# Last feed-forward part: seven 2x2 block products in place of eight for 19 of 22 tile pairs, and inner activations in four parts

## The chip, the cores and the metric

The kernel runs on one core of one Trainium2 chip. The metric is the device time of one execution in microseconds (us), the median of the runs shown. The core has TensorE (matrix products, weights loaded beside them), VectorE (DVE), ScalarE (ACT), GpSimd (POOL) and a queue for transfers (SyncE, SP). They run at the same time and each takes its own instructions in order; they wait for each other through semaphores.

## What is computed

The kernel computes two models one after the other on 528 token columns (16 meta tokens and 512 others), later 512 with 256 context tokens: one hybrid layer (feed-forward, retention and attention, feed-forward), then two layers "latent" (0 and 1) with attention and a feed-forward part. The change touches the last feed-forward part, that of latent layer 1, and what feeds it. Cut to this, the reference is

```
def swiglu(x, w_in, w_out):
    a, b = jnp.split(x @ w_in, 2, axis=-1)
    return (jax.nn.silu(a) * b) @ w_out
# h: 512 tokens x 1024; x = modulated layer norm of h; w_in: 1024 x 5632; w_out: 2816 x 1024
# h = layer norm of (h + gate * swiglu(x, w_in, w_out))
```

All products are of float32 values split into a high and a low part: high x high + high x low + low x high, three matmuls for each block of 128 x 128 weights.

## The kernel before, in words

**Layout.** Everything is held transposed, features on the 128 partitions and tokens along the row. Model width 1024 is 8 blocks (k = 0 to 7), the inner width 2816 is 22 tiles (j = 0 to 21). A "pair" j is the tile of a ("fa", then silu) and that of b ("fb", then the gating a*b). The 512 tokens are two halves ("chunks" in the code) of 256 columns, c = 0 and 1. One tile for one half is 8 blocks x 3 matmuls of 256 columns = 24 matmuls (`tile_item`, line 1210, and `mm3`, line 1136, whose three matmuls are lines 1137 to 1139).

**A weight's way.** `SyncE.weight` (3433) loads a tile of 128 x 1024 numbers (512 KB) into one of NW = 4 raw buffers `Wf`; it waits until the buffer's earlier content has been split. `ScalarE.split` (1761, the copy is line 1770) writes the rounded high part into one of six slots (three "base", three "top"), `VectorE.split` (2397, line 2403) subtracts it from the raw weight and writes the low part. Then TensorE may use it. How far ahead ScalarE and VectorE split is `Engine.ahead` (1055): tiles up to `used + look`, only into slots whose earlier tile is finished. Since each engine's instructions are in order, a split stands in its queue at the place where `ahead` gave it out.

**A pair's way.** TensorE makes fa and fb; ScalarE takes silu of fa from PSUM (1971); VectorE multiplies by fb from PSUM (`gated`, 2647, line 2652); ScalarE writes the high part of the result to `H3h` (`hidden_high`, 1980, line 1987); GpSimd subtracts and writes the low part to `H3l` (`PoolE.step`, 3190, line 3197).

**Parts.** The inner activations are kept for 8, 7 and 7 pairs at a time (`CH`, line 20). After each part the 8 output tiles m ("fo") are made, nj blocks each, and VectorE adds them to the residual `H` (`residual`, 2655, line 2664). The part's buffers are used again by the next one. In the first two parts a tile serves both halves in turn; after the third part half 0 gets its 8 output tiles first, then half 1, each with its weights loaded and split anew (`Ffn.ends`, 516).

**Order.** `latent_sequence` (823) makes the list of steps, and `woven` (706) puts the steps of the norms (`chain`, 668) between them by planned times (0.345 us per block). A `Group` (684) gives out the tiles of both halves, the one furthest behind first, with one at most 5 tiles ahead: so half 0 goes ahead while the norm of half 1 is still made. In this layer `look` is 3 throughout. `FILL` (629) puts filler matmuls (line 1125) into known waits of TensorE. The norm in front (b1 and c1) ends with ScalarE's scaled activations `XC` (1948) and high part `X2h` (1951), and low parts `X2l` by VectorE (2628, blocks 0 to 3) and GpSimd (3240, blocks 4 to 7). The norm behind (d1) runs for half 0 during the output tiles of half 1: sums by TensorE (1341, 1363), ScalarE's and VectorE's part, then ScalarE's writes to `H` (1964) and the stores.

PSUM has 8 banks, taken in turn (`take`, 1095); a bank is free once the operation that read it is done.

## Time and profile before

| | |
|---|---|
| median of 3 runs | 3349.62 us (3346.73 to 3352.74) |
| span of the profiled execution, first to last instruction | 3342.8 us |
| difference of the two, what lies around the span | 6.8 us |
| TensorE busy in the profile | 3245.9 us |
| last feed-forward part, first matmul to last | 2936.1 to 3324.3 us |

The profile is of one execution; its times are from the span's start. A group line gives an operation's output and inputs, its shape, how often it occurs, its busy time in total and the mean of one, then the idle time of its engine before it and what ended that. A matmul is recorded with its whole passage (0.28 us); as the next one enters before it is out, they follow each other more closely than that. A few matmul records are missing from the trace. The granted clock is 1.00 at 2.4 GHz and 0.50 at 1.2 GHz.

### The profile page before, as it was taken

To read this page: it belongs to the slowest core of one execution; us is meant where nothing else is said; L and a number is where in the kernel's file an instruction comes from. 1 tells how busy PE (TensorE), PEld (TensorE's weight loads), DVE (VectorE), ACT (ScalarE), POOL (GpSimd) and SP (SyncE) were. 2 spreads that over 40 slices of the span, in tenths; PEclk is the share of its full clock that TensorE was granted. 3 is DMA by queue.
4 is the path that set the end of the run, shared out by engine and by line. 5 is a ranking of instruction groups with operands and counts; after the bars stand their busy time and mean duration, and the time that the engine had idled before them with its cause. 6 is when DMAs were issued, how large, how long until landed. Compare 5 with 4: busy or idle time off the path is not lost. (4 is left out here: it accounts for less than half of the span.)

```text
span 3342.8 us, 59968 instructions
## 1 busy us (share of the span) xinstructions
PE 3245.9 (97%) x24670; PEld 3027.7 (91%) x24686; DVE 1693.8 (51%) x2839; ACT 1329.2 (40%) x2350; POOL 474.2 (14%) x471
## 2 busy tenths in 40 slices
PE   8999999999999999999999999999999999999998
PEld 7999988887778999999789889999998889889997
DVE  4666643546634456665545773222227646743334
ACT  4222222346633432225348663112125547552224
POOL 1010010036400010011013201001010114110100
PEclk9999999999999999999999999999999999999999
DMA  4444422122122344453201421111223212422222
GB/s 162 161 171 171 144 83 70 59 77 60 55 82 95 101 141 169 171 176 110 66 20 42 133 91 64 58 63 58 64 65 125 92 50 54 148 71 95 89 92 92
DMA packets 94973, 325.23 MB, mean 97 GB/s; under 512 B 10800, under 2 KB 15152, under 8 KB 94576
## 3 DMA queue, kind: packets, MB, share of 16 engines
q1 hardware_dynamic: 90992, 307.19, 28.0%
q0 software_dynamic: 3280, 13.68, 1.2%
q8 instruction: 199, 3.26, 0.4%
q14 instruction: 70, 0.57, 0.1%
q10 hardware_dynamic: 432, 0.52, 0.0%
HBM read 309.96 MB, written 2.10 MB: 93 GB/s over the span
## 5 line engine op out<-in xcount | busy, mean ns | idle before, releaser
L2403 DVE TENSOR_TENSOR r_Wbasel<-r_Wf,r_Wbaseh 128x1024 fp32r<-128x1024 f32 (+1 forms) x298 | 380.0, 1277 | 536.3 <-ACT r_Wbaseh L1770 535.9
L1770 ACT ACTIVATE r_Wbaseh<-r_Wf 128x1024 fp32r<-128x1024 f32 (+1 forms) x298 | 307.9, 1037 | 438.8 <-PE PS L1139 340.1
L1137 PE MATMUL PS<-r_X1h,r_Wbaseh 128*128 128x264 f32 (+2 forms) x1216 | 391.0, 322 | 13.0 <-DVE r_X1l L2644 3.7
L1137 PE MATMUL PS<-r_X2h,r_Wbaseh 128*128 128x256 f32 (+1 forms) x1224 | 373.4, 305 | 4.9 <-POOL r_X2l L3240 2.5
L1138 PE MATMUL PS<-r_X1l,r_Wbaseh 128*128 128x264 f32 (+2 forms) x1216 | 377.0, 310 | 0.0
L1139 PE MATMUL PS<-r_X1h,r_Wbasel 128*128 128x264 f32 (+2 forms) x1216 | 376.7, 310 | 0.0
L1139 PE MATMUL PS<-r_X2h,r_Wbasel 128*128 128x256 f32 (+1 forms) x1224 | 366.8, 300 | 0.0
L1138 PE MATMUL PS<-r_X2l,r_Wbaseh 128*128 128x256 f32 (+1 forms) x1224 | 364.1, 297 | 0.0
L2403 DVE TENSOR_TENSOR r_Wtopl<-r_Wf,r_Wtoph 128x1024 fp32r<-128x1024 f32 (+1 forms) x165 | 200.1, 1214 | 274.1 <-ACT r_Wtoph L1770 274.0
L1137 PEld LDWEIGHTS PS<-r_X1h,r_Wbaseh 128*128 128x128 f32 x1216 | 228.9, 188 | 35.7 <-issue 8.1
L1137 PE MATMUL PS<-r_X2h,r_Wtoph 128*128 128x256 f32 x872 | 248.6, 285 | 1.7 <-POOL r_X2l L3240 1.2
L1138 PE MATMUL PS<-r_X2l,r_Wtoph 128*128 128x256 f32 x872 | 248.0, 284 | 0.0
L1139 PE MATMUL PS<-r_X2h,r_Wtopl 128*128 128x256 f32 x872 | 247.9, 284 | 0.0
L1137 PEld LDWEIGHTS PS<-r_X2h,r_Wbaseh 128*128 128x128 f32 x1224 | 230.4, 188 | 18.3 <-POOL r_X2l L3240 3.3
L1138 PEld LDWEIGHTS PS<-r_X1l,r_Wbaseh 128*128 128x128 f32 x1216 | 229.4, 189 | 13.9 <-issue 2.4
L1138 PEld LDWEIGHTS PS<-r_X2l,r_Wbaseh 128*128 128x128 f32 x1224 | 232.3, 190 | 10.4 <-issue 2.6
L1139 PEld LDWEIGHTS PS<-r_X1h,r_Wbasel 128*128 128x128 f32 x1216 | 229.5, 189 | 12.5
L1139 PEld LDWEIGHTS PS<-r_X2h,r_Wbasel 128*128 128x128 f32 x1224 | 229.6, 188 | 7.8
L1770 ACT ACTIVATE r_Wtoph<-r_Wf 128x1024 fp32r<-128x1024 f32 (+1 forms) x165 | 168.4, 1025 | 164.7 <-PE PS L1139 84.0
L1977 ACT ACTIVATE r_TM<-PS 128x256 f32<-128x256 f32 (+1 forms) x198 | 75.8, 384 | 339.4 <-PE PS L1139 334.7
L1137 PE MATMUL PS<-r_X1h,r_Wtoph 128*128 128x264 f32 (+1 forms) x672 | 190.7, 284 | 4.9 <-DVE r_Wtopl L2403 4.9
L2652 DVE TENSOR_TENSOR r_TM<-r_TM,PS 128x256 f32<-128x256 f32 (+1 forms) x198 | 83.3, 420 | 213.6 <-PE PS L1139 202.4
(428 smaller groups left out, 9058.3 us busy)
## 6 DMA issues: line engine op xcount, KB each, us to landing
r_Wf<-in_wmod SPq DMA_DIRECT2D x96, 512.0 KB, 3.6
r_Wf<-in_f_in SPq DMA_DIRECT2D x88, 512.0 KB, 4.4
r_Wf<-in_g_in SPq DMA_DIRECT2D x88, 512.0 KB, 3.5
r_Wf<-in_g_out SPq DMA_DIRECT2D x56, 448.0 KB, 3.3
r_Wf<-in_w_o SPq DMA_DIRECT2D x40, 512.0 KB, 4.4
r_Wf<-in_f_out SPq DMA_DIRECT2D x32, 448.0 KB, 4.2
r_Wf<-in_f_out SPq DMA_DIRECT2D x16, 512.0 KB, 4.4
r_Wf<-in_w_v SPq DMA_DIRECT2D x16, 512.0 KB, 3.5
```

What stands on the lines that cost most here:

```text
L1137: self.e.matmul(o, wh, xh, start=first, stop=False)
L1138: self.e.matmul(o, wh, xl, start=False, stop=False)
L1139: return self.e.matmul(o, wl, xh, start=False, stop=last)
L1770: e.activation(p.w(i, cols)[0], p.Wf[:, i % NW, 0:cols], ACT.Copy).then_inc(*p.hi.did(i))
L1977: e.activation(f.tm(c), p.psb(p.bank(("fa", f.tag, j, c)), f.chunks[c][1]), ACT.Silu).then_inc(*p.act.did(("silu", f.tag, j, c)))
L2403: e.tensor_tensor(l, p.Wf[:, i % NW, 0:cols], h.bitcast(F32), ALU.subtract).then_inc(*p.lo.did(i))
L2652: e.tensor_tensor(x, x, p.psb(p.bank(("fb", f.tag, j, c)), f.chunks[c][1]), ALU.mult).then_inc(*p.dve.did(("gated", f.tag, j, c)))
```

## The change

**Products.** For pairs 3 to 21 of this part the weights of a pair are taken as a 2x2 block matrix: A11 and A12 are the halves of the tile of a (k 0 to 3 and 4 to 7), A21 and A22 those of b. In the code the second load is called B where it is summed (B[:, 0:512] is A21, B[:, 512:1024] is A22). The activations are a 2x2 block matrix as well, block(row half, token half). The eight block products become seven, on sums of blocks: S1 to S4 of weights, T1 to T4 of activations. Each product is 4 blocks x 3 = 12 matmuls of 256 columns. A weight half-tile of 128 x 512 that a product needs is a "unit".

- GpSimd makes the four sums S of each pair from the raw weights (step "sums", parts 0 to 2 = S1 and S2, S3, S4). S is one buffer each, freed when VectorE has made the low part of the unit of the pair before.
- ScalarE and VectorE split units of 512 in place of tiles of 1024, up to 7 works ahead (`units_ahead`) into 12 half slots.
- In place of silu from PSUM and the gating: ScalarE copies four intermediate results out of PSUM ("kept" 0, 2, 3, 4, after products 0, 2, 3, 4), VectorE adds three times (sum1, sum3, sum2), ScalarE takes silu twice from SBUF, and VectorE gates one half with PSUM and one with SBUF. Product 2 goes on in the bank of product 0 and waits for kept 0; product 4 waits for kept 2, product 5 for kept 3, product 6 for kept 4.
- "combine" makes T1 to T4 once: three block differences of 128 x 1024 on VectorE and one on GpSimd; when all four are done ScalarE makes four high parts (over the raw activations), then VectorE three low parts and GpSimd one.

**Order.** The first two pairs run as before (a group of 4 tiles, 5 ahead at most); then come `look` = 1, the sums of pair 3, combine, `units_ahead` = 7, then pair 2 in the old way with both halves in turn, then the products. The gating and low parts of pair j come after product 0 of pair j+1.

**Parts.** For this layer the inner activations are in parts of 5, 5, 6 and 6 pairs; between them output tiles in the old way with half 1 two tiles behind.

The rest of the diff widens `CH` to `CHS` by layer, moves this layer's buffers, and leaves the other three feed-forward parts as they are. Its core:

```diff
+CHS = {"f1": CH, "f2": CH, "g0": CH, "g1": [(0, 5), (5, 5), (10, 6), (16, 6)]}
+PLAIN_PAIRS = 3
+UNITS_AHEAD = 7
...
+PRODUCTS = [("A11", "B11", "a", None), ("A12", "B21", "c", None), ("S2", "T2", "a", 0), ("S1", "T1", "b", None),
+            ("S3", "T3", "a", 2), ("S4", "B22", "b", 3), ("A22", "T4", "a", 4)]
...
+    nc, plain = len(f.chunks), 2 * PLAIN_PAIRS
+    items = [Group(tiles[:plain - 2], range(nc), 5, lambda c: c), (("ahead", 1), 0, None),
+             *[(("sums", f, PLAIN_PAIRS, x), 0, None) for x in range(3)], (("combine", f), 0, None),
+             (("units_ahead", UNITS_AHEAD), 0, None), Group(tiles[plain - 2:plain], range(nc), 1, lambda c: c)]
+    chs = CHS[f.tag]
+    for ci, (j0, nj) in enumerate(chs):
+        j1 = j0 + nj - 1
+        for j in range(max(j0, PLAIN_PAIRS), j0 + nj):
+            for i in range(7):
+                items.append((("product", f, j, i), 1.45, None))
+                if j < j1 and i == 0:
+                    items.append((("sums", f, j + 1, 1), 0, None))
+                    if j == max(j0, PLAIN_PAIRS):
+                        items.insert(-1, (("sums", f, j + 1, 0), 0, None))
+                if i == 0 and j > max(j0, PLAIN_PAIRS):
+                    items.append((("hidden", f, j - 1), 0, None))
+                if j < j1 and i == 2:
+                    items.append((("sums", f, j + 1, 2), 0, None))
+                if j < j1 - 1 and i == 5:
+                    items.append((("sums", f, j + 2, 0), 0, None))
+                if j == j1 and i in (2, 4, 6):
+                    items.append((("ahead", i // 2 - 1), 0, None))
+        items.append((("hidden", f, j1), 0, None))
+        if ci == len(chs) - 1:
+            break
+        for (what, (ci, m), nk), c in lagged([x for x in tiles if x[0][0] == "fo" and x[1][0] == ci], nc, 2):
+            items.append((("fo", f, (ci, m), c), 0.345 * nk, None))
+            if c == 0 and m >= 5:
+                items.append((("sums", f, j1 + 1, m - 5), 0, None))
+        items.append((("ahead", -1), 0, None))
+    items.append((("ahead", 3), 0, None))
+    return items
...
-    items.append(Group(tiles, range(nc), 5, lambda c: c))
-    items += [(("fo", f, (2, m), c), 2.4, None) for c in range(nc) for m in range(8)]
+    if l == 0:
+        items.append(Group(tiles, range(nc), 5, lambda c: c))
+    else:
+        items += fast_items(f, tiles)
+    items += [(("fo", f, (last, m), c), 0.345 * CHS[f.tag][last][1], None) for c in range(nc) for m in range(8)]
...
+        works, before = self.p.works, self.p.before
+        while self.next < len(works):
+            x = works[self.next]
+            if x[0] == "w" and x[1] > self.used + self.look:
+                return
+            if x[0] == "unit" and self.next > self.reached + self.units_ahead:
+                return
+            if any(b not in self.fin for b in before[x]):
+                return
+            if x[0] == "w":
+                self.split(x[1])
+            else:
+                self.split_unit(x)
...
+        if kept is None:
+            freed = {"a": ("gated", tag, j, 0), "c": ("sum1", tag, j), "b": ("sum2", tag, j)}[bank]
+            b = self.take(("product", tag, j, bank), (p.dve, freed))
+        else:
+            b = p.bank(("product", tag, j, bank))
+            e.wait_ge(*p.act.of(("kept", tag, j, kept)))
+        e.wait_ge(*p.lo.of(key))
+        if moving[0] == "T":
+            e.wait_ge(*(p.pool if moving == "T3" else p.dve).of(("combined", tag, moving)))
+        wh, wl = p.unit(key)
+        for k in range(4):
+            xh, xl = f.operand(moving, k)
+            h, l = wh[:, 128 * k:128 * k + 128], wl[:, 128 * k:128 * k + 128]
+            more = kept is not None
+            e.matmul(p.psb(b, n), h, xh, start=k == 0 and not more, stop=False, skip_group_check=more)
+            e.matmul(p.psb(b, n), h, xl, start=False, stop=False, skip_group_check=more)
+            t = e.matmul(p.psb(b, n), l, xh, start=False, stop=k == 3, skip_group_check=more)
+        t.then_inc(*p.mm.did(("product", tag, j, i), key))
...
+        self.begin_product(f, j, i)
+        if i in (2, 6):
+            c = i // 4
+            e.wait_ge(*p.dve.of((("sum1", "sum2")[c], tag, j)))
+            e.activation(f.tm(j, c), f.tm(j, c), ACT.Silu).then_inc(*p.act.did(("silu", tag, j, c)))
+        if i in (0, 2, 3, 4):
+            e.wait_ge(*p.mm.of(("product", tag, j, i)))
+            if i in (0, 2):
+                e.wait_ge(*p.pool.of(("hid", tag, j - 2, i // 2)))
+            elif j > PLAIN_PAIRS:
+                e.wait_ge(*p.dve.of(("sum3", tag, j - 1) if i == 3 else ("gated", tag, j - 1, 1)))
+            e.activation(f.kept(j, i), p.psb(p.bank(("product", tag, j, PRODUCTS[i][2])), n), ACT.Copy).then_inc(
+                *p.act.did(("kept", tag, j, i)))
...
+        for i in (0, 1):
+            e.wait_ge(*p.dve.of(("low", N.id, i, 0)))
+            e.wait_ge(*p.pool.of(("low", N.id, i, 1)))
+        for t in (2, 1, 3, 4):
+            e.wait_ge(*p.dve.of(("blocks", f.tag, 4)))
+            e.wait_ge(*p.pool.of(("blocks", f.tag, 3)))
+            e.activation(f.TH[:, t - 1], f.TR[:, t - 1], ACT.Copy).then_inc(*p.act.did(("blocks_high", f.tag, t)))
...
+        self.begin_product(f, j, i)
+        if i == 1:
+            e.wait_ge(*p.act.of(("kept", tag, j, 0)))
+            e.wait_ge(*p.mm.of(("product", tag, j, 1)))
+            e.tensor_tensor(f.tm(j, 0), f.tm(j, 0), p.psb(p.bank(("product", tag, j, "c")), n), ALU.add).then_inc(
+                *p.dve.did(("sum1", tag, j)))
+        if i == 5:
+            e.wait_ge(*p.act.of(("kept", tag, j, 4)))
+            e.tensor_tensor(f.kept(j, 4), f.kept(j, 4), f.kept(j, 3), ALU.add).then_inc(*p.dve.did(("sum3", tag, j)))
+            e.wait_ge(*p.mm.of(("product", tag, j, 5)))
+            e.tensor_tensor(f.tm(j, 1), f.tm(j, 1), p.psb(p.bank(("product", tag, j, "b")), n), ALU.add).then_inc(
+                *p.dve.did(("sum2", tag, j)))
...
+        T = [f.TR[:, t] for t in range(4)]
+        e.tensor_tensor(T[0], f.block(1, 2), f.block(1, 1), ALU.subtract).then_inc(*p.dve.did(("blocks", tag, 1)))
+        e.wait_ge(*p.dve.of(("blocks", tag, 1)))
+        e.tensor_tensor(T[1], f.block(2, 2), T[0], ALU.subtract).then_inc(*p.dve.did(("blocks", tag, 2)))
+        e.wait_ge(*p.dve.of(("blocks", tag, 2)))
+        e.tensor_tensor(T[3], f.block(2, 1), T[1], ALU.subtract).then_inc(*p.dve.did(("blocks", tag, 4)))
+        for t in (2, 1, 4):
+            e.wait_ge(*p.act.of(("blocks_high", tag, t)))
+            e.tensor_tensor(f.TL[:, t - 1], T[t - 1], f.TH[:, t - 1].bitcast(F32), ALU.subtract).then_inc(
+                *p.dve.did(("combined", tag, f"T{t}")))
...
+        if part == 0:
+            if p.pool.known:
+                e.wait_ge(*p.w_arrived(a))
+                e.wait_ge(*p.w_arrived(b))
+            freed(3)
+            e.tensor_tensor(S[:, 0, :], B[:, 0:512], B[:, 512:1024], ALU.add).then_inc(
+                *p.pool.did(("sum", tag, j, "S1")))
+            freed(2)
+            e.wait_ge(*p.pool.of(("sum", tag, j, "S1")))
+            e.tensor_tensor(S[:, 1, :], S[:, 0, :], A[:, 0:512], ALU.subtract).then_inc(
+                *p.pool.did(("sum", tag, j, "S2")))
+        elif part == 1:
+            freed(4)
+            e.tensor_tensor(S[:, 2, :], A[:, 0:512], B[:, 0:512], ALU.subtract).then_inc(
+                *p.pool.did(("sum", tag, j, "S3")))
+        else:
+            freed(5)
+            e.wait_ge(*p.pool.of(("sum", tag, j, "S2")))
+            e.tensor_tensor(S[:, 3, :], A[:, 512:1024], S[:, 1, :], ALU.subtract).then_inc(
+                *p.pool.did(("sum", tag, j, "S4")))
...
+        T = f.TR[:, 2]
+        e.tensor_tensor(T, f.block(2, 2), f.block(1, 2), ALU.subtract).then_inc(*p.pool.did(("blocks", tag, 3)))
+        e.wait_ge(*p.act.of(("blocks_high", tag, 3)))
+        e.tensor_tensor(f.TL[:, 2], T, f.TH[:, 2].bitcast(F32), ALU.subtract).then_inc(
+            *p.pool.did(("combined", tag, "T3")))
```

## Rows read from the trace of the kernel before

**Rows 1.** Page, part 1: busy time, share of the span, instructions of each engine.

```profile
PE 3245.9 (97%) x24670; PEld 3027.7 (91%) x24686; DVE 1693.8 (51%) x2839; ACT 1329.2 (40%) x2350; POOL 474.2 (14%) x471
```

**Rows 2.** Stretch of the last feed-forward part: us, busy (instructions) by engine, clock, DMA.

```profile
3084.00:3162.00 78.00, 78.00 (x652) 78.00 (x651) 21.44 (x28) 23.82 (x42) 10.36 (x14) 1.00 0.26 82
```

**Rows 3.** TensorE's waits from 2940 us on: total us, times, longest.

```profile
PE PS L1137 <- POOL r_X2l L3240: 1.2, 1, 1.2
...
PE PS L1137 <- DVE r_X2l L2628: 0.5, 1, 0.5
```

**Rows 4.** Groups by shape in 2960 to 3320 us: busy us, mean ns, idle before.

```profile
L3197 POOL TENSOR_TENSOR r_H3l<-r_TM,r_H3h 128x256 fp32r<-128x256 f32 x43 | 31.8, 740 | 291.5 <-ACT r_H3h L1987 291.5
...
L2403 DVE TENSOR_TENSOR r_Wtopl<-r_Wf,r_Wtoph 128x1024 fp32r<-128x1024 f32 x24 | 29.4, 1223 | 56.5 <-ACT r_Wtoph L1770 56.5
...
L1770 ACT ACTIVATE r_Wtoph<-r_Wf 128x1024 fp32r<-128x1024 f32 x24 | 25.2, 1052 | 26.0 <-PE PS L1139 26.0
...
L2652 DVE TENSOR_TENSOR r_TM<-r_TM,PS 128x256 f32<-128x256 f32 x43 | 18.1, 421 | 59.0 <-PE PS L1139 55.9 <-ACT r_TM L1977 3.1
L1987 ACT ACTIVATE r_H3h<-r_TM 128x256 fp32r<-128x256 f32 x43 | 18.0, 418 | 93.4 <-DVE r_TM L2652 93.4
...
L2403 DVE TENSOR_TENSOR r_Wtopl<-r_Wf,r_Wtoph 128x896 fp32r<-128x896 f32 x11 | 12.0, 1087 | 12.7 <-ACT r_Wtoph L1770 12.7
L1770 ACT ACTIVATE r_Wtoph<-r_Wf 128x896 fp32r<-128x896 f32 x11 | 10.2, 945 | 5.0 <-PE PS L1139 5.0
```

**Rows 5.** Timeline of VectorE and GpSimd, 464 to 468 us: start, us taken, instruction.

```profile
464.91 0.69 DVE L2698 TENSOR_TENSOR r_RT<-PS,r_CS 128x512 f32<-128x512 f32 x1 [3.58 <-PE PS L1444]
465.63 1.71 DVE L2403 TENSOR_TENSOR r_Wbasel<-r_Wf,r_Wbaseh 128x1024 fp32r<-128x1024 f32 x1
467.26 0.68 DVE L2705 TENSOR_TENSOR r_RQ<-r_RQ,r_RT 128x512 f32<-128x512 f32 x1
...
464.95 1.30 POOL L3247 TENSOR_TENSOR r_RQ<-r_RQ,r_CS 128x512 f32<-128x512 f32 x1 [5.39 <-PE PS L1444]
```

**Rows 6.** Timeline at the part's start, 2950 to 2958 us: TensorE, VectorE, GpSimd.

```profile
2950.65 1.46 PE L1125 MATMUL PS<-r_CF 128*128 128x256 f32 x6
...
2956.79 0.39 PE L1137 MATMUL PS<-r_X2h,r_Wtoph 128*128 128x256 f32 x1 [1.23 <-POOL r_X2l L3240]
...
2955.28 2.53 DVE L2403 TENSOR_TENSOR r_Wtopl<-r_Wf,r_Wtoph 128x1024 fp32r<-128x1024 f32 x1 [2.78 <-ACT r_Wtoph L1770]
...
2954.39 2.35 POOL L3240 TENSOR_TENSOR r_X2l<-r_XC,r_X2h 128x1024 fp32r<-128x1024 f32 x1 [18.89 <-ACT r_X2h L1951]
```

**Rows 7.** Timeline, 656 us (VectorE, GpSimd) and 721 us (GpSimd alone).

```profile
656.46 1.22 DVE L2403 TENSOR_TENSOR r_Wbasel<-r_Wf,r_Wbaseh 128x1024 fp32r<-128x1024 f32 x1
...
656.63 1.95 POOL L3294 TENSOR_TENSOR r_RS<-r_RS 128x512 f32<-128x512 f32 x1 [17.08 <-DVE r_RS L2874]
...
720.87 1.04 POOL L3294 TENSOR_TENSOR r_RS<-r_RS 128x512 f32<-128x512 f32 x1 [5.25 <-DVE r_RS L2874]
```

**Rows 8.** Stretches before this part, as in rows 2; the clock is third from last.

```profile
2926.00:2929.00 3.00, 0.64 (x8) 0.19 (x8) 2.96 (x3) 2.97 (x6) 0.00 (x0) 0.90 0.00 0
2929.00:2932.00 3.00, 2.88 (x25) 1.15 (x26) 1.72 (x2) 2.98 (x6) 0.00 (x0) 0.53 0.00 0
```

**Rows 9.** Timeline of a plain tile's end, 3087 to 3090 us: TensorE, VectorE, GpSimd.

```profile
3087.76 0.28 PE L1139 MATMUL PS<-r_X2h,r_Wtopl 128*128 128x256 f32 x1
...
3088.15 0.42 DVE L2652 TENSOR_TENSOR r_TM<-r_TM,PS 128x256 f32<-128x256 f32 x1 [0.36 <-PE PS L1139]
...
3089.09 0.74 POOL L3197 TENSOR_TENSOR r_H3l<-r_TM,r_H3h 128x256 fp32r<-128x256 f32 x1 [53.95 <-ACT r_H3h L1987]
```

**Rows 10.** Timeline of the end, 3321 to 3327 us: TensorE and ScalarE.

```profile
3324.34 1.38 PE L1341 MATMUL PS<-r_H,r_CF 128*32 128x256 f32 x16
...
3321.86 4.05 ACT L1964 ACTIVATE r_H<-r_H,r_V 128x256 f32<-128x256 f32 x8 [2.74 <-DVE r_H L2640]
3325.82 0.36 ACT L1884 ACTIVATE r_PA<-PS 128x256 f32<-128x256 f32 x1
```

## What the change does to the time: the prediction

> **What bounds the kernel now.** I read the page first: TensorE is busy 97% of the span, no other engine above 51% [rows 1]. The last feed-forward part runs from 2936 us to 3324 us. In the table by stretch, 78 us of it hold 652 matmul records and no idle time [rows 2], so a matmul of 256 columns takes a place of 0.120 us. TensorE's waits [rows 3] say that after the first tiles it waits for nothing in this part. A feed-forward matmul taken away is worth its 0.120 us, as long as nothing new makes TensorE wait. ScalarE, VectorE and GpSimd work beside it; their durations are in [rows 4]. The times of a 128x512 operation are in [rows 5]: 0.68 us on VectorE, 1.30 us on GpSimd. ScalarE's weight copy of 512 elements is 0.62 us by the slope between its 896 and 1024 elements.
>
> **A row that decides much.** VectorE and GpSimd are not independent. The weight subtraction L2403 takes 1.22 us alone, but started under a GpSimd product it ended 1.09 us after that product's end [rows 5], and likewise in [rows 6], where it took 2.53 us. The other way round, a GpSimd operation that takes 1.04 us took 1.95 us, ending 0.90 us after VectorE's [rows 7]. A VectorE operation with one input in PSUM ran its usual 0.69 us beside GpSimd [rows 5]. So two operations that each read SBUF twice (GpSimd's all) run one after the other; the blocked one saves only 0.13 us. This is also the rule in the Trainium skill, page "SBUF — State Buffer", section "Who interferes with whom": VectorE with two SBUF inputs and GpSimd reading SBUF exclude each other for the whole instruction. The trace agrees.
>
> **Removed.** Per pair 8 block products of 12 matmuls become 7, in 19 pairs: 228 x 0.120 = -27.4 us. (By the Trainium skill, page "TensorE: Matmul & The Clock Gate", section "Back-to-back issue gap", N/2.4 + 2.5 ns, a matmul would be 0.109 us and this -24.9 us; the row of 0.120 is used.) The four inner parts have the same matmuls as the three.
>
> **Chunk 0's head start.** Half 0 of the tokens now runs 5 tiles while half 1's norm is made, up to 2950.5; then filler and waits, until GpSimd's low part lets TensorE go on at 2956.8 [rows 6]. The new first group has 4 tiles. That chain is not TensorE's, so one tile of 24 matmuls is missing as cover: +2.9 us.
>
> **The combination of the activations** (steps "sums", "combine", "units_ahead"). All of it stands in the queues behind the last plain tile of pair 1; call TensorE's end of that tile 0. TensorE has 11.5 us of pair 2 to do. GpSimd: low of pair 1, four sums, then its block difference. VectorE: three block differences, each 1.22. ScalarE's four copies wait for both, since they overwrite the raw activations. With every SBUF operation in turn: VectorE's differences end at 1.8, 3.5, 5.8; GpSimd's low at 2.4, sums at 4.7, 6.9, 8.3, 9.7, difference (2.35) at 12.1. Copies end 13.2 to 16.1. VectorE's lows end at 14.5 and 15.6; GpSimd's (2.35) at 17.8; VectorE's third at 18.9. Only then come the eight weight lows of the look-ahead, 0.56 apart: the first at 19.5, so product 0 of pair 3 starts 8.0 us late. The last ends at 23.3, the two gatings of pair 2 at 24.0, their ScalarE copies at 24.5, a weight copy and the kept copy of product 0 at 25.3: product 2, due at 22.4, starts 3.0 late. Then GpSimd's two lows and sums 1 and 2 of pair 4 (to 28.8), the copy and low of that sum (30.8), sum1, silu and the second kept copy (31.8): product 4, due at 28.1, is 3.6 late. Together +14.6 us. After 3 us in which TensorE was busy for 0.64, the granted clock was 0.53 over the next 3 us, that is 1.2 GHz instead of 2.4 for nearly all of them [rows 8]. After 8 us of idle time it will be low too; half of such a stretch is lost: +1.6.
>
> **A full pair.** TensorE needs 84 x 0.120 = 10.1 us. Beside it, VectorE: 7 weight lows of 0.68, one sum and one gating of 0.42 from SBUF (5.6 us), and three operations with PSUM. GpSimd: 4 sums of 1.30, 2 lows of 0.74 (6.7 us). Taken one by one that is 12.3 us; with 0.13 hidden on each of the 15, 10.3 us. So a full pair costs between 10.1 and 12.3 us, and what matters is which waits for which. In the queues: late in a pair, sums 1 to 3 alternate with the weight lows in front of sum2 on VectorE; sum2 ends 2.0 us into the next pair, silu1, a weight copy and kept copy 0 behind it at 3.3: product 2, due at 2.9, is 0.5 late. The gatings come at 4.4, the copies 4.8, GpSimd's lows 6.1, sum 4 at 7.8, interleaved with the weight low before sum1 (7.0); silu0 and kept copy 2 end at 7.8: product 4, due at 6.2, is 1.6 late. A pair takes 12.1 us. How many are full? Over the output tiles of the part before, GpSimd makes the sums of a part's first two pairs and 8 weight units are split; the last two pairs have no sums left to make. Full are 2 pairs of the part of five and 3 of each part of six: 8 x 2.05 = +16.4 us. The others cost nothing: the output tiles' own weights take ScalarE and VectorE under 2 us of 3.6.
>
> **The parts' ends**, now four. At each, the first output tile needs the last pair's low. Tiles of half 1 covered this before. Now behind the last product come silu1 (held up by an output weight's low in front of sum3 and sum2), an output weight's copy and low, gating, copy, GpSimd's low: the chain of [rows 9], 1.9 us, with 1.4 us more, 3.3 us in all. Four or five k-steps cover 1.4 to 1.8: 1.3 + 3 x 2.0 = +7.3 us.
>
> **The tail.** Half 1's last output tiles shrink from 20.2 to 17.3 us while half 0's norm goes on. TensorE and ScalarE now arrive at the last norm together, 3325.7 and 3325.8 [rows 10]; the norm's TensorE steps move up by 2.2 us of the 2.9. The rest is left: +0.7. Sixteen more residual additions are hidden under output tiles. Loads carry the same bytes; two of 512 KB per 10 to 12 us, against two per 11.5 before, are hidden.
>
> Sum: -27.4 + 2.9 + 14.6 + 1.6 + 16.4 + 7.3 + 0.7 = +16.1 us. The profiled span of 3342.8 becomes 3358.9; the median stands 6.8 above the span, so 3365.7 us. About 0.2% (6.7 us) is what a measurement can tell from no change.
>
> **Rivals.** (A) SBUF operations hardly get into each other's way, because they fall apart in time. Then full pairs cost 10.1 us. At the start GpSimd's difference ends at 9.9, the fourth copy at 13.9, VectorE's third low at 15.1, the first weight low at 15.7: product 0 is 4.2 late, products 2 and 4 then 3.3 and 2.8, together 10.3 instead of 14.6. Sum: -27.4 + 2.9 + 10.3 + 1.6 + 7.3 + 0.7 = -4.6, so 3345 us. For it: today both engines are active at once seldom and lose little. Against: [rows 5 to 7], and 12.3 us of such work in 10.1. (B) Faster: the kept copies are in time. ScalarE has 7.5 us of work in a pair of 10.1; if it reaches kept copy 2 before 5.8 us of the pair, TensorE never waits in a pair, not even in pair 3 after its first product (4.2 late, as in A), nor at a part's end beyond the first (1.3). -27.4 + 2.9 + 4.2 + 1.3 + 0.7 = -18.3, 3331 us. For it: ScalarE's load. Against: its queue is in order, and silu0 stands before that copy. (C) Worse: a blocked operation hides nothing and each hand-over costs, so full pairs take 3.4 us over and first pairs 1.0: about +30, 3380 us. (D) The matmuls don't get fewer because each stop at a product boundary costs TensorE 0.1 us more: 133 x 0.1 = +13 on top of the sum; the tile boundaries within [rows 2] show none, so this has little weight.
>
> **Numbers.** Chances: my forecast 0.45, C and D together 0.13, A 0.22, B 0.20. The range takes the forecast's bounds (start 10 to 17, full pairs 8 to 25: 3352 to 3377) and A, and leaves B's and C's far ends out: 3335 to 3377; the forecast's own is 3352 to 3377. Faster by over 0.2%: B and a third of A, 0.25. Within: most of A and the forecast's lower edge, 0.20. Slower: 0.55.
>
> **What would show it.** Right: TensorE idle of 7 to 9 us once near 2980 us, before the first product; a fall of granted clock there; VectorE weight lows of 128x512 with a mean well above 0.68 us, and GpSimd sums above 1.30; TensorE waits at products 2 and 4 for ScalarE's copies, some 2 us per pair in the middle of each part; about 2 us before the first output tile of each part; 228 fewer matmuls. Wrong: waits of TensorE in this part under 10 us in all, or lows of 0.7 us though GpSimd runs beside them. (A) would show the second, (B) both and ScalarE's kept copies never as what a product waited for; (C) pairs of 13 us. I would also be wrong if the first pairs of the parts were as late as the middle ones.

## The result, and the profile after

| | before | after |
|---|---|---|
| median, same chip | 3348.29 us (3346.73 to 3352.74, 4 runs) | 3368.68 us (3364.26 to 3371.06, 4 runs) |
| ratio, 95% interval | | 1.0053 [1.0041, 1.0065] |
| span of the profiled execution | 3342.8 us | 3362.4 us |
| last feed-forward part, first matmul to last | 388.3 us | 402.4 us |

The changed kernel is 0.5% slower: 20.4 us by the medians, 17.7 by the ratio (13.7 to 21.8), where 16.1 were forecast; 3368.7 us where 3365.7 were. It lies inside the range, on the forecast's side. (In every run the time is 1.9 us above the span of that execution. The 6.8 us called "what lies around the span" above are these 1.9 and 4.9 by which the profiled execution before was shorter than the median.)

The page's first part, after, to be set beside [rows 1]:

```profile
PE 3235.2 (96%) x24458; PEld 3010.7 (90%) x24458; DVE 1813.4 (54%) x3021; ACT 1391.4 (41%) x2533; POOL 597.2 (18%) x549
```

TensorE is busy for 10.7 us less, and the span is 19.6 us longer. (212 of the 228 matmuls show; a few records are missing on either side.) VectorE took on 120 us of work, GpSimd 123.

TensorE's waits from 2940 us on, after (what waited and for what: us in total, times, longest), beside [rows 3]:

```profile
PE PS L1367 <- ACT r_TM L2006: 15.7, 18, 3.2
PE PS L1367 <- DVE r_Wtopl L2668: 7.7, 1, 7.7
PE PS L1296 <- POOL r_H4l L3546: 6.9, 4, 2.0
PE PS L1296 <- DVE r_X3la L2945: 3.3, 1, 3.3
```

Line 1367 is a block product's first matmul, 1296 a plain tile's; `r_TM` by line 2006 is a kept copy, 2668 a unit's low part, 3546 the low part of the inner activations. They are the waits of the forecast: the kept copies 18 times (16 in eight full pairs, two in pair 3), the first product once, the parts' ends four times, the head start once. 33.6 us of waits stand where [rows 3] have 1.7.

The start of the block products (timeline of TensorE, after; lines 1298 and 1296 are plain tiles; in brackets the idle time just before and what ended it):

```profile
2982.17 0.28 PE L1298 MATMUL PS<-r_X3h,r_Wtopl 128*128 128x256 f32 x1
2990.15 0.55 PE L1367 MATMUL PS<-r_X3h,r_Wtoph 128*128 128x256 f32 x1 [7.69 <-DVE r_Wtopl L2668]
...
2996.17 0.39 PE L1367 MATMUL PS<-r_TH,r_Wtoph 128*128 128x256 f32 x1 [1.10 <-ACT r_TM L2006]
```

Stretches at that place, after (us, busy of each engine with instructions, granted clock third from last):

```profile
2984.00:2987.00 3.00, 0.00 (x0) 0.00 (x0) 2.52 (x3) 3.00 (x5) 1.32 (x1) 1.00 0.00 0
2987.00:2990.00 3.00, 0.00 (x0) 0.00 (x0) 3.00 (x3) 3.00 (x7) 1.32 (x1) 0.57 0.00 0
2990.00:2993.00 3.00, 2.85 (x13) 2.88 (x14) 3.00 (x6) 1.24 (x4) 0.00 (x0) 0.50 0.38 107
2993.00:2996.00 3.00, 2.07 (x13) 1.86 (x11) 2.00 (x6) 1.42 (x4) 0.93 (x2) 0.79 0.34 112
```

Product 0 starts 7.9 us after it was due (8.0 forecast), and the granted clock is at 1.2 GHz behind the idle time. At that clock most of products 0 and 1 runs, and takes longer. So product 2, which starts 3.1 us later than 24 matmuls at 0.120 us would have it (3.0 forecast), stands still for only 1.1 of them. Product 4, at 3002.49, starts 3.4 us later than product 2 would have it (3.6 forecast) and waits 3.2.

One full pair (VectorE and GpSimd, then TensorE's stretches of 12 us, after):

```profile
3062.26 3.75 DVE L2668 TENSOR_TENSOR r_Wtopl<-r_SR,r_Wtoph 128x512 fp32r<-128x512 f32 x3
3063.88 1.58 POOL L3563 TENSOR_TENSOR r_SR<-r_Wf 128x512 f32<-128x512 f32 x1 [0.72 <-DVE r_Wtopl L2668]
3065.60 1.56 POOL L3567 TENSOR_TENSOR r_SR<-r_SR,r_Wf 128x512 f32<-128x512 f32 x1
3065.93 1.78 DVE L2668 TENSOR_TENSOR r_Wtopl<-r_Wf,r_Wtoph 128x512 fp32r<-128x512 f32 x1
3067.12 1.74 POOL L3571 TENSOR_TENSOR r_SR<-r_Wf 128x512 f32<-128x512 f32 x1
3067.63 1.51 DVE L2682 TENSOR_TENSOR r_TM<-r_TM,r_TM 128x256 f32<-128x256 f32 x1
3069.07 0.41 DVE L2684 TENSOR_TENSOR r_TM<-r_TM,PS 128x256 f32<-128x256 f32 x1
```

```profile
3071.00:3083.00 12.00, 10.58 (x86) 10.18 (x86) 10.49 (x13) 6.43 (x15) 7.98 (x6) 1.00 0.18 56
```

VectorE's sum3 (line 2682), 0.42 us of work, took 1.51 beside GpSimd's sum; the sum from PSUM right behind it (2684) took its 0.41. TensorE's waits at products 2 and 4 repeat with the same 0.2 and 1.22 us in eight pairs, and the two rows below stand one pair apart, 12.01 us for 84 matmuls:

```profile
3075.12 0.39 PE L1367 MATMUL PS<-r_TH,r_Wtoph 128*128 128x256 f32 x1 [1.22 <-ACT r_TM L2006]
...
3087.13 0.38 PE L1367 MATMUL PS<-r_TH,r_Wbaseh 128*128 128x256 f32 x1 [1.22 <-ACT r_TM L2006]
```

Groups by shape, 2960 to 3345 us, after (busy us, mean ns):

```profile
L2668 DVE TENSOR_TENSOR r_Wtopl<-r_SR,r_Wtoph 128x512 fp32r<-128x512 f32 x44 | 43.8, 1017 | 10.0 <-ACT r_Wtoph L1989 9.2
```

The low parts have a mean of 1.02 us where [rows 5] have 0.68 for such an operation alone.

### The profile page after: what moved, and what is told of

It reads as the page before. It is cut to its first block and busy times, and to the rows that moved or that the text cites. A ratio compares the mean times of both kernels' runs of the same rounds, so it can differ in the third digit from the quotient of the medians.

```text
span 3362.4 us, 60358 instructions
## 1 busy us (share of the span) xinstructions
PE 3235.2 (96%) x24458; PEld 3010.7 (90%) x24458; DVE 1813.4 (54%) x3021; ACT 1391.4 (41%) x2533; POOL 597.2 (18%) x549
## 5 line engine op out<-in xcount | busy, mean ns | idle before, releaser
L2661 DVE TENSOR_TENSOR r_Wbasel<-r_Wf,r_Wbaseh 128x1024 fp32r<-128x1024 f32 (+3 forms) x286 | 360.8, 1263 | 512.0 <-ACT r_Wbaseh L1975 511.6
L1975 ACT ACTIVATE r_Wbaseh<-r_Wf 128x1024 fp32r<-128x1024 f32 (+3 forms) x286 | 290.8, 1021 | 427.0 <-PE PS L1298 322.3
L2661 DVE TENSOR_TENSOR r_Wtopl<-r_Wf,r_Wtoph 128x1024 fp32r<-128x1024 f32 (+3 forms) x147 | 174.5, 1188 | 211.6 <-ACT r_Wtoph L1975 211.5
L1296 PE MATMUL PS<-r_X2h,r_Wbaseh 128*128 128x256 f32 (+1 forms) x888 | 278.6, 314 | 3.7 <-DVE r_Wbasel L2661 1.8
L1298 PE MATMUL PS<-r_X2h,r_Wbasel 128*128 128x256 f32 (+1 forms) x888 | 271.7, 306 | 0.0
L1297 PE MATMUL PS<-r_X2l,r_Wbaseh 128*128 128x256 f32 (+1 forms) x888 | 269.8, 304 | 0.0
L1975 ACT ACTIVATE r_Wtoph<-r_Wf 128x1024 fp32r<-128x1024 f32 (+3 forms) x147 | 145.8, 1000 | 142.3 <-PE PS L1298 62.8
L1297 PE MATMUL PS<-r_X1l,r_Wtoph 128*128 128x264 f32 (+1 forms) x672 | 190.6, 284 | 0.0
L1298 PE MATMUL PS<-r_X1h,r_Wtopl 128*128 128x264 f32 (+1 forms) x672 | 190.3, 283 | 0.0
L1296 PE MATMUL PS<-r_X2h,r_Wtoph 128*128 128x256 f32 x504 | 143.5, 285 | 0.0
```

What stands on the lines that cost most here:

```text
L1296: self.e.matmul(o, wh, xh, start=first, stop=False)
L1297: self.e.matmul(o, wh, xl, start=False, stop=False)
L1298: return self.e.matmul(o, wl, xh, start=False, stop=last)
L1975: e.activation(p.w(i, cols)[0], p.Wf[:, i % NW, 0:cols], ACT.Copy).then_inc(*p.hi.did(i))
L2661: e.tensor_tensor(l, p.Wf[:, i % NW, 0:cols], h.bitcast(F32), ALU.subtract).then_inc(*p.lo.did(i))
```

## The experiments

Each kernel is the changed one with one edit, but for one that starts from the kernel before. They were timed beside the kernel before in three groups, in which that kernel had 3351.13 us (with the kernels of sums written with three pieces, VectorE's sums first, a later start and output weights sooner), 3350.62 (29 pieces, filler) and 3351.57 (the others). So ratios to it are compared: the changed kernel's is 1.0053.

**Sums not read, only written.** GpSimd's four sums of a pair are left out and the buffers filled with a constant, in three pieces. The order of the steps stays. (What the kernel computes is then not the reference's; the same holds for the next two.)

```diff
-            e.tensor_tensor(S[:, 0, :], B[:, 0:512], B[:, 512:1024], ALU.add).then_inc(
+            for q in (0, 176):
+                e.memset(S[:, 0, q:q + 176], 0.25).then_inc(*p.pool.did(("piece", tag, j, 0, q)))
+            e.memset(S[:, 0, 352:512], 0.25).then_inc(
```

(likewise S2, S3 and S4)

> The four weight sums of each pair are left out; GpSimd writes their buffers in three constant pieces each instead, so it is about as long busy but reads nothing from SBUF (the results are not the reference's). Theory (operations of VectorE and GpSimd that read SBUF run one after the other): VectorE's 128x512 weight lows come back from 0.84 to 1.02 us to about 0.7, a pair in the middle of a part takes 10.1 to 10.4 us instead of 12.0, the eight waits of 1.22 and of 0.20 us for ScalarE's kept copies go, the wait before the first product falls from 7.7 to about 5.5 us; in all 15 to 20 us less than the changed kernel: 3349 to 3354 us. Rival (GpSimd's sums are simply late in its own queue, whatever they read): with the same busy time of GpSimd nothing changes, 3368 us and waits of 1.22 us as before.

Measured 3343.67 us, 0.9982 [0.9973, 0.9991], so 24 us less than the changed kernel where 15 to 20 were expected. All 16 waits of the full pairs are gone, and the waits at the parts' ends (6.9 in 4) and of the head start (3.3) are as they were. TensorE's waits from 2940 us on, and one group by shape, of this kernel:

```profile
PE PS L1367 <- ACT r_TM L2006: 2.6, 2, 1.7
...
L2668 DVE TENSOR_TENSOR r_Wtopl<-r_SR,r_Wtoph 128x512 fp32r<-128x512 f32 x44 | 32.9, 758 | 16.7 <-ACT r_Wtoph L1989 16.6
```

But the edit did two things: three pieces take 0.60 us in all, where a sum takes 1.49 to 1.67 (means of the four sums in the changed kernel). The expectation had called that "about as long", and this is why more was gained than expected: with 29 pieces, below, it is 18 us. Either VectorE no longer stood still, or GpSimd was no longer late. The next two runs part these.

**As long, still only written.** 13 pieces, then 29, for each buffer. The lines for 29 against those for three, shortened (each buffer's last piece of 8 columns is not shown):

```diff
-            for q in (0, 176):
-                e.memset(S[:, 0, q:q + 176], 0.25)...
+            for q in range(0, 504, 18):
+                e.memset(S[:, 0, q:q + 18], 0.25)...
```

> The four sums of a pair on GpSimd are left out and each buffer of sums is written with a constant in 13 pieces (12 of 40 columns, one of 32) instead of 3, so that GpSimd is busy for about as long as with the sums (13 pieces at about 0.10 to 0.13 us are 1.3 to 1.7 us for each; the sums took 1.5 to 1.67) while it reads nothing from SBUF. Theory (the wait in each full pair comes from VectorE's two-input operations on SBUF standing still while GpSimd's run): the full pairs keep no wait, as with the short writes; low parts of 128x512 at 0.69 to 0.77 us; 3343 to 3346 us. Rival (the sums are simply late, since GpSimd is busy too long, and the short writes took that away): the waits of some 2 us in each of 8 full pairs return, 15 us, and the time is 3356 to 3361 us.

> As the run with 13 pieces, but each buffer of sums is written with 29 pieces (28 of 18 columns, one of 8): the 13 pieces took only 0.94 us where the sums take 1.49 to 1.67, since their starts stood 0.066 to 0.073 us apart; of such a start 0.042 us is the columns and about 0.03 us is fixed, so 18 columns come to 0.05 us and 29 pieces to about 1.5 us. Theory (VectorE's operations on two SBUF inputs stand still beside GpSimd's sums): still no wait in any full pair, low parts of 128x512 at 0.69 to 0.77 us; about as the 13 pieces, 3346 to 3350 us. Rival (GpSimd is late): 0.8 us or more of waiting comes back in each of 8 full pairs, over 6 us, and ScalarE's high parts are seen waiting for the buffers of sums: 3354 to 3360 us.

With 13 pieces 3348.34 us, 0.9992 [0.9983, 1.0001]; with 29, 3350.34 us, 0.9999 [0.9990, 1.0008]. GpSimd's timeline with 29 pieces, two groups of VectorE's, and TensorE over one pair:

```profile
3069.08 1.45 POOL L3570 MEMSET r_SR<- 128x18 f32 x28
...
3070.50 1.26 POOL L3576 MEMSET r_SR<- 128x18 f32 x28
```

```profile
L2668 DVE TENSOR_TENSOR r_Wtopl<-r_SR,r_Wtoph 128x512 fp32r<-128x512 f32 x44 | 32.9, 759 | 16.7 <-ACT r_Wtoph L1989 16.6
...
L2682 DVE TENSOR_TENSOR r_TM<-r_TM,r_TM 128x256 f32<-128x256 f32 x19 | 8.0, 419 | 4.2 <-ACT r_TM L2006 4.2
```

```profile
3065.00:3075.08 10.08, 10.08 (x86) 10.08 (x86) 6.85 (x12) 6.51 (x16) 6.75 (x119) 1.00 0.22 67
```

With 29 pieces GpSimd is busy for 1.3 to 1.5 us a buffer, as long as a sum of 1.30 that nothing holds up [rows 5], and still no full pair has a wait: a pair takes 10.08 us, and sum3 0.42. So the "late GpSimd" rival falls for the full pairs. Taken one by one in that trace, from 2996 us on, the 48 low parts of 128x512 that ran beside constant writes took 0.69 us in the mean, the 63 with GpSimd idle 0.69 as well, and the 11 beside GpSimd's own low parts, which read two inputs, 1.21: it is such ones that lift the group's mean to 0.76. What blocks VectorE is an operation of GpSimd that reads SBUF, not one that writes it. (The edit also puts another instruction in the place of the sums; a GpSimd operation that reads only one input was not tried. Nor do the runs part whether VectorE's delay or the sums' own, 1.57 us in the mean for 1.30, does more of it.) This is what the Trainium skill, page "SBUF — State Buffer", section "Who interferes with whom", says: VectorE with two SBUF inputs contends with a GpSimd instruction that reads SBUF, not with one that only writes it; the groups at 759 and 419 ns agree. (By the Trainium skill, page "TensorE: Matmul & The Clock Gate", section "Back-to-back issue gap", a matmul of 256 columns has a gap of 0.109 us, and the undisturbed pair would be an estimated 84 x 0.109 = 9.2 us; the row has 10.08. The page gives that gap for an isolated matmul and says that in a stream with weight loads the load helps to set the spacing. Every matmul here has its load, so the prediction's -24.9 us took the wrong one of the two.)

At the start GpSimd's length does count: product 0 waited 3.0, 4.3 and 5.9 us with 3, 13 and 29 pieces, and 7.7 with the sums. The expectations had left this out: 3348.3 lies above its 3343 to 3346, and 3350.3 just above its 3346 to 3350. By product 4 of pair 3 the three kernels are 7.5, 9.4 and 12.0 us late, which gives 1.9 and 4.5 us of the 3.4 and 5.7 us by which the ratios of 13 and 29 pieces lie above that of three. What is left is within the intervals and was not parted; the profiled executions with 13 and with 29 pieces also show 1.2 GHz behind a wait of 1.84 us where the one with three pieces does not (below).

**VectorE's sums first.** In its steps 1 and 5 VectorE makes sum1, and sum3 with sum2, before the low part of a weight that stood in front of them.

```diff
-        self.begin_product(f, j, i)
+        if i not in (1, 5):
+            self.begin_product(f, j, i)
...
+        if i in (1, 5):
+            self.begin_product(f, j, i)
         self.end_product(f, j, i)
```

> On VectorE alone the sums of the intermediate results (sum1; sum3 and sum2) stand in front of the weight low of the same step, not behind it; nothing is left out. Theory (what costs is that silu and so the kept copies stand behind sums that stand behind a blocked weight low): full pairs take 10.2 to 11.2 us instead of 12.0, the first full pair of a part nothing, about 12 us less in all: 3357 us (3353 to 3361). Rival (the shared port is simply full, so that the order within the queue matters little): pairs of 11.5 us or more, 3364 us or more.

Measured 3355.93 us, 1.0018 [1.0009, 1.0026]. The kept copies' waits fall from 15.7 us in 18 to

```profile
PE PS L1367 <- ACT r_TM L2006: 7.6, 7, 2.1
```

with the same GpSimd sums beside VectorE. The time lies within the expected 3353 to 3361. Only five of the eight full pairs still wait, some 1.0 us each by the distance of their matmuls' starts, 5 us in place of 15.4. So the collisions make VectorE late, but it is the order of its queue that lets most of this reach TensorE.

**A later start.** Pairs 3 and 4 are plain too, so 17 pairs are left as block products. The block differences follow pair 2, their high and low parts pair 3, the first group has 6 tiles, and the first sums of weights come under the output tiles of the first part.

```diff
-PLAIN_PAIRS = 3
+PLAIN_PAIRS = 5
...
-    items = [Group(tiles[:plain - 2], range(nc), 5, lambda c: c), (("ahead", 1), 0, None),
-             *[(("sums", f, PLAIN_PAIRS, x), 0, None) for x in range(3)], (("combine", f), 0, None),
-             (("units_ahead", UNITS_AHEAD), 0, None), Group(tiles[plain - 2:plain], range(nc), 1, lambda c: c)]
+    items = [Group(tiles[:plain - 4], range(nc), 5, lambda c: c), (("blocks", f), 0, None),
+             Group(tiles[plain - 4:plain - 2], range(nc), 1, lambda c: c), (("combine", f), 0, None),
+             Group(tiles[plain - 2:plain], range(nc), 1, lambda c: c), (("ahead", 2), 0, None),
+             (("units_ahead", UNITS_AHEAD), 0, None)]
```

> Five pairs in the old way instead of three (17 pairs with products); block differences after pair 2, high and low parts after pair 3, and the first pair's sums under the output tiles of the first part; the first group has 6 tiles. Costs 2 x 12 x 0.120 = 2.9 us of matmuls. Theory (the start costs because everything stands in one heap before pair 3): the waits of 7.7, 1.1 and 3.2 us go, so do the 2 x 1.7 us of low clock behind them, one tile of head start (2.9) comes back and the first part's end (1.2) is covered again: 19 to 20 less, 3 more, so 16 less in all: 3353 us (3348 to 3358). Rival (the heap only moves, and the weights of the second part come late instead): 3362 us or more, with new waits before the first product of the second part.

Measured 3352.08 us, 1.0007 [0.9998, 1.0015], as expected (3353), though it removes 24 matmuls fewer. The 7.7 us are gone, the head start's waits are back at 0.5 and 1.2, and the full pairs wait as before:

```profile
PE PS L1369 <- ACT r_TM L2008: 11.4, 16, 1.2
PE PS L1298 <- POOL r_H4l L3558: 5.8, 3, 2.0
...
PE PS L1298 <- POOL r_X3lb L3626: 1.2, 1, 1.2
```

**The output weights split sooner.** At a part's end the first three output weights are given out to be split after products 0, 1 and 2 of the last pair, not 2, 4 and 6.

```diff
-                if j == j1 and i in (2, 4, 6):
-                    items.append((("ahead", i // 2 - 1), 0, None))
+                if j == j1 and i in (0, 1, 2):
+                    items.append((("ahead", i), 0, None))
```

> In the last pair of each part the first three output weights are released for splitting after products 0, 1 and 2 instead of 2, 4 and 6. Theory (the wait at a part's end is the chain silu, split, gating, copy, low, with one output weight's split inside it and one in front of the sums): the four waits for GpSimd's low part, 1.2 + 1.8 + 2.0 + 2.0 us, fall to 0.2 to 0.5 us each, 5 to 6 us less in all: 3363 us (3360 to 3366). Rival (the chain of gating, copy and low alone is longer than the k-steps that cover it): waits of 1.5 us or more stay, 3367 us or more.

Measured 3359.36 us, 1.0029 [1.0019, 1.0039], 0.6 us below the expected 3360 to 3366; the parts' ends wait 1.2 us in 2 where it was 6.9 in 4. The output weights' splits had stood in front of the last sums and the gating, as the forecast's chain had it.

**GpSimd's difference before its sums.** At the start GpSimd makes its block difference ahead of the three steps "sums" of pair 3.

```diff
+             (("third", f), 0, None),
              *[(("sums", f, PLAIN_PAIRS, x), 0, None) for x in range(3)], (("combine", f), 0, None),
```

(The rest of the edit takes that difference out of "combine" into a step of its own.)

> GpSimd makes its block difference of the inputs ahead of the three sums of pair 3 rather than behind them; nothing else moves. If the start of the block products waits for GpSimd's difference behind its sums, the 7.7 us before product 0 shrink by the about 5 us that the sums take, to 3 us: 3364 us or less. If it is VectorE's own queue (combinations and weight lows, slowed by whatever GpSimd runs beside it) that ends last, the same work collides in another order and 0 to 2 us go: 3366 to 3369 us.

Measured 3365.57 us, 1.0044 [1.0032, 1.0057], between the two branches. The wait before product 0 falls by 1.6 us only, not to 3 us, and that before product 4 stays:

```profile
2987.62 0.55 PE L1368 MATMUL PS<-r_X3h,r_Wtoph 128*128 128x256 f32 x1 [6.13 <-DVE r_Wtopl L2669]
2993.64 0.46 PE L1368 MATMUL PS<-r_TH,r_Wtoph 128*128 128x256 f32 x1 [0.56 <-ACT r_TM L2007]
2999.95 0.39 PE L1368 MATMUL PS<-r_TH,r_Wbaseh 128*128 128x256 f32 x1 [3.11 <-ACT r_TM L2007]
```

So of the 14.4 us of the start 1.6 were GpSimd's order. The wait still ends with VectorE's first weight low, and 1.6 us less is what the second branch had.

**Filler in the first wait.** 34 matmuls right ahead of product 0 of pair 3, into its bank, columns 256 to 511. The product itself writes columns 0 to 255 of it, and nothing reads the filler's half. (The expectation has it that the product clears that half; what is computed is unchanged either way.)

```diff
             b = self.take(("product", tag, j, bank), (p.dve, freed))
+            if (j, i) == (PLAIN_PAIRS, 0):
+                for _ in range(34):
+                    e.matmul(p.PS[:, b, 256:512], p.ONES, p.CF[:, 0:2, :], start=True, stop=True)
```

> The changed kernel with 34 matmuls more, into a part of the accumulator that product 0 of the first pair clears again, right ahead of that product: they fill about 4 of the 7.7 us in which TensorE stands still there. What it computes is unchanged. If the granted clock fell because TensorE stood still, products 0 and 1 of that pair now run at the full clock, but product 2 needs the kept copy of product 1 and VectorE's queue is as late as before, so that what the clock gives back returns as a longer wait before product 2: 3367 to 3370 us, no change. Rival: the low clock costs its 3.4 us on the path: 3364 to 3366 us.

Measured 3369.10 us, 1.0059 [1.0047, 1.0072]: no change from the changed kernel. The dose was larger than meant. The filler's operands are plain float32 and not of the products' rounded type (fp32r); the 34 calls show as 68 matmuls and took 14.5 us, not 4 (timeline of TensorE, then two stretches):

```profile
2983.67 14.84 PE L1358 MATMUL PS<-r_CF 128*128 128x256 f32 x68
2998.16 0.47 PE L1370 MATMUL PS<-r_X3h,r_Wtoph 128*128 128x256 f32 x1
```

```profile
2990.00:2993.00 3.00, 3.00 (x16) 2.64 (x15) 3.00 (x5) 2.63 (x7) 0.00 (x0) 1.00 0.01 3
...
2999.00:3002.00 3.00, 3.00 (x27) 3.00 (x27) 0.28 (x1) 1.33 (x3) 2.86 (x3) 1.00 0.00 0
```

So product 0 began 14.5 us after it was due instead of 7.9, and the end came no later: at the full clock no product of pair 3 waits any more, and product 4 starts 14.49 + 48 x 0.120 = 20.3 us after the plain tile's end; in the changed kernel it was 3002.49 - 2982.29 = 20.2. So 6.6 us more before product 0 cost nothing. The trace of the changed kernel says why, and that the low clock costs nothing there either (GpSimd, ScalarE, VectorE, after):

```profile
2998.33 1.28 POOL L3567 TENSOR_TENSOR r_SR<-r_SR,r_Wf 128x512 f32<-128x512 f32 x1
...
2999.64 0.63 ACT L1989 ACTIVATE r_Wbaseh<-r_SR 128x512 fp32r<-128x512 f32 x1 [3.52 <-POOL r_SR L3567]
...
3000.30 1.08 DVE L2668 TENSOR_TENSOR r_Wbasel<-r_SR,r_Wbaseh 128x512 fp32r<-128x512 f32 x1 [3.27 <-ACT r_Wbaseh L1989]
```

Product 4 waits for kept copy 2, that for silu and sum1, sum1 stands behind this low part, and the low part waits through ScalarE for GpSimd's second sum of pair 4. Neither product 0 nor product 1 is in that chain. Before it stand GpSimd's two lows of pair 2 (from 2995.07), ScalarE's copies for them (2994.58), VectorE's gatings (2994.14) and, in front of these in VectorE's queue, the eight weight lows. The start is worth what shortens this chain, and not what fills the wait.

**Four parts alone.** The kernel before, with this layer's inner activations in parts of 5, 5, 6 and 6.

```diff
+CHS = {"f1": CH, "f2": CH, "g0": CH, "g1": [(0, 5), (5, 5), (10, 6), (16, 6)]}
```

(The rest of the edit puts `CHS` for `CH` where the parts are counted.)

> The kernel before with one part of the change alone: the inner activations of this feed-forward part in four parts (5, 5, 6 and 6 tiles) instead of three; all products plain. Theory: the parts cost nothing by themselves while their ends are hidden (waits at part ends only appear with the block products, whose short last products leave GpSimd no room), so 3348 to 3351 us, the same as before. Rival: each part end costs the 2 us seen in the changed kernel whatever the products are, one more end and no room in any: 3352 to 3356 us.

Measured 3352.37 us, 1.0002 [0.9993, 1.0010]: the same within its interval. No part's end shows a wait, and the feed-forward part is as long as before, 388.3 us. So the parts' ends cost nothing without block products in front of them. But what is behind the part grew by 1.7 us in the profile, just as in the changed kernel; the median's interval is too wide to show it. TensorE in the last norm (the kernel before, then this one):

```profile
3326.32 0.67 PE L1363 MATMUL PS<-r_PA,r_CF 128*128 128x256 f32 x2 [0.60 <-ACT r_PA L1884]
3326.83 2.32 PE L1125 MATMUL PS<-r_CF 128*128 128x256 f32 x10
```

```profile
3333.03 0.67 PE L1365 MATMUL PS<-r_PA,r_CF 128*128 128x256 f32 x2 [1.39 <-ACT r_PA L1886]
3333.54 4.01 PE L1127 MATMUL PS<-r_CF 128*128 128x256 f32 x10
```

Half 0's norm ends 1.1 us later against the last output tile, and the ten filler matmuls behind the longer wait ran at 1.2 GHz.

**The three edits together** (later start, VectorE's sums first, output weights released sooner).

> All three edits at once: two more plain pairs' worth of room before the first block product (the block differences and sums run under the tiles of pairs 3 and 4 of the plain order and the first sums stand under plain tiles), VectorE makes the kept copies' sum1 and sum3 ahead of the weight's low part, and the output weights are released after products 0, 1 and 2 of the last pair of a part. Theory: each wait has one cause of its own (start: the order of the combine heap; full pairs: the kept copy behind a slowed low part; part ends: GpSimd's output lows begun too late), so the gains add: the single edits gave 3368.7 - 3352.1 = 16.6, 3368.7 - 3355.9 = 12.8 and 3368.7 - 3359.4 = 9.3 us, sum 38.7: 3330 us, with waits of about 8 to 10 us left from 2940 on. Rival: the causes share an engine, and what one edit takes off VectorE or GpSimd the next finds missing, so that the combination is worth no more than the two largest, about 29 us: 3340 us, with waits of over 18 us left. The kernel before is at about 3350, so by either theory this one is faster than it.

Measured 3335.31 us, 0.9954 [0.9941, 0.9966]: faster than both kernels. The three single gains against 1.0053 are 0.0046, 0.0035 and 0.0024; taken from it together they give 0.9948, within the interval. The two largest alone give 0.9972, just outside; with the intervals of the single runs the times by themselves do not rule that rival out, and 3335.3 lies halfway between its 3340 and the theory's 3330. The waits decide it: 6.4 us of them in the feed-forward part, where the theory left 8 to 10 and the rival over 18. TensorE's waits from 2940 us on:

```profile
PE PS L1369 <- ACT r_TM L2008: 4.3, 5, 0.9
...
PE PS L1298 <- POOL r_X3lb L3629: 1.2, 1, 1.2
PE PS L1298 <- DVE r_X3la L2958: 0.5, 1, 0.5
PE PS L1298 <- POOL r_H4l L3561: 0.4, 1, 0.4
```

## Why the prediction was right, step by step

Against the forecast's terms, from the profiled execution after. "Late" is the start of a matmul against where it was due at 0.120 us from the one before.

| term | forecast | measured |
|---|---|---|
| head start of half 0 | +2.9 | +3.3: waits 3.3 for 1.7, and 1.7 of low clock (34 us at 0.95 for 1.00) |
| start of the block products, clock with it | +16.2 | +14.4: product 4 begins at 3002.49, due at 2988.05 |
| eight full pairs | +16.4 | +15.4: 12.00 us a pair less 10.08, eight times |
| parts' ends | +7.3 | +7.6 |
| tail | +0.7 | +1.7: waits 1.0 longer, 0.7 of low clock |
| matmuls removed | -27.4 | not measured by itself |

With -27.4 these make 15.0 against the forecast's 16.1. The part grew by 402.4 - 388.3 = 14.1 us and what is behind it by 1.7, together 15.8, so 0.8 stay unassigned. That the sum is so near is in part luck: the start and the full pairs were put 2.8 us too high, the other three terms 1.7 too low. The remaining 3.8 of the 19.6 us by which the spans differ lie ahead of the part, in code that the change leaves alone: its first plain tile starts at 2939.84 in place of 2936.07. Stretches of low clock account for them (below).

**The mechanism** was the forecast's: VectorE and GpSimd, where each reads SBUF twice, run one after the other. The run with 29 pieces shows it for the full pairs, at about equal length of GpSimd's work. Rival (A) fell on this, and on 1.02 us for 0.68. Its world, GpSimd busy as long but in nobody's way, is nearest to that kernel: the full pairs are without a wait, and product 4 of pair 3 is 12.0 us late, where (A) had 10.3 and 1.6 for the clock. It had 3350.3 us where (A) gave 3345; 3.4 us of the difference are low clock behind two parts' ends in its profile. The kernel with three pieces came out at 3343.7, but with far less work on GpSimd, so that its nearness to 3345 is chance. Rival (B) fell on 18 waits for kept copies. Rival (C), nothing hidden, on pairs of 12.0 us and not 13.5. Rival (D) fell on the undisturbed pair: 10.08 us for seven products leave nothing for boundaries.

**The start** came as its chain was worked out: product 0 late by 7.9 us (forecast 8.0), product 2 by 3.1 more (3.0) and product 4 by 3.4 more (3.6). The 1.6 us added for the clock was the wrong step. The low clock took its time out of the wait before product 2, and the chain to product 4 does not pass through the products that ran slowly, so the term should have been 0. **The tail** was mis-sized by 1.0 us. The run with four parts alone has the whole 1.7 without any block product, so it belongs to the shorter last part: ScalarE ended half 0's norm 1.1 us later against the last output tile, where the forecast had 0.7, and 0.7 more is filler at 1.2 GHz. In six of the nine other profiles of kernels with four parts that low clock is missing, and what is behind the part grew by 1.0 us.

**Slips in the working.** For the parts' ends a chain of 3.3 us less a cover of 1.4 to 1.8 gives 1.5 to 1.9 us each, 6.8 in all; the sum used 1.3 and three times 2.0 instead. The waits were 1.2, 1.8, 2.0 and 2.0, so the figures used are right and the working for them is not. (B) and a third of (A) make a chance of 0.27, not 0.25.

**The queue's order** was in the forecast's working but not said as plainly as the runs say it: the full pairs' wait is the collision's only because low parts stand ahead of sum1 and sum3. Either is enough to take most of it away: no reads, or two steps swapped.

## What to carry to other kernels

An exchange of TensorE work for VectorE and GpSimd work is priced by the chain through the queues of those engines, with their SBUF operations laid end to end, and not by their busy shares: 54% and 18% here, and TensorE waited 33.6 us. When such a wait repeats at the same size in each round, look first at what stands ahead of the late operation in its own in-order queue: two swapped steps were worth 0.35%, and with a later start (two pairs fewer as block products) and the splits sooner as well the change went from 0.5% slower to 0.5% faster. A wait is only worth what the next one behind it lets through: fill or shorten it and see whether the end moves.

## What the runs showed of the hardware that was not expected

**The clock is sometimes low behind a wait of 1.8 us and sometimes not.** Behind the end of the second part, where TensorE waited 1.84 us before 3095.31, the kernel with 13 pieces shows

```profile
3090.00:3100.00 10.00, 8.16 (x56) 7.96 (x55) 6.51 (x11) 3.90 (x8) 1.42 (x2) 0.83 0.46 127
```

that is 1.7 us lost to 1.2 GHz, while the changed kernel's wait of 1.84 us before 3105.06 has none behind it. In code that the change leaves alone the changed kernel's execution, then the one before, have

```profile
2600.00:2610.00 10.00, 8.45 (x63) 6.67 (x64) 6.32 (x6) 6.41 (x11) 0.00 (x0) 0.83 0.33 105
```

```profile
2600.00:2610.00 10.00, 10.00 (x80) 9.80 (x79) 6.85 (x7) 6.34 (x12) 1.44 (x1) 1.00 0.33 107
```

behind the same two waits in the norm there, 1.2 to 1.3 and 1.8 us. Up to 2930 us such stretches took 10.2 us in the one execution and 5.9 in the other (each stretch of 10 us times what its clock lacks of 1), which is about the 3.8 us above. Over all twelve profiles it was 2.1 to 13.7 us. So two single profiles of this kernel can differ by up to 0.3% through this alone, and the times go with it: of the kernel before, an execution of 3345.69 us had a mean clock of 0.997 and one of 3356.26 us a mean clock of 0.993. Why the clock falls in one execution and not in another stays open; whether the kept waits of the changed kernel bring more of it in the median was not tested.

**Small constant writes on GpSimd are cheap to start:** 28 of 18 columns took 1.26 to 1.45 us in all, so 0.045 to 0.052 us each, where 13 pieces of 40 and 32 columns came to 0.92 us, 0.07 each. From these two, as an estimate, a column adds some 1 ns and each piece some 0.03 us whatever its size.
